# First two down parts of a feed-forward stage as seven products of half blocks

## The chip, the cores and the metric

One NeuronCore of a Trainium2 chip runs the whole program. The metric is the device time of one execution in microseconds (us), lower is better.

## The reference, cut to what matters

A vector of 512 tokens by 1024 features passes through eight stages: feed-forward (stages 0, 2, 3, 5, 7) and mixers (1, 4, 6). The change concerns the feed-forward stages, which all compute

```
def swiglu_ffn(x, norm, w_gate, w_up, w_down):
    h = rms_norm(x, norm)
    return (jax.nn.silu(h @ w_gate) * (h @ w_up)) @ w_down
```

with `x = x + 0.5 * swiglu_ffn(...)` in four of them and a factor of 1 in the last. The hidden width is 2816. Everything is fp32. The kernel reaches that precision with three fp32r products for each product: an operand is split into a high part (rounded to fp32r) and a low part (the rest), and high by high, low by high and high by low are summed in PSUM.

## The kernel before, in words

**Queues.** Each engine's instructions are written by Python generators that yield a planned time ("tick", one tick is three matmuls of 512 columns) before each step; `weave` merges the generators of an engine in order of these ticks. So the yields set the order of an engine's instructions, and nothing else: what starts when is decided on the chip by semaphores.

**Weights.** A weight chunk is 512 KB (128 partitions by 1024 fp32) in one of 12 buffers (`k_raw`, `k_xraw`). SyncE's queue loads it. Before use it is split: ScalarE writes the high part (`k_wh` or `k_xwh`, L842 in `act_weights`), VectorE the rest (`k_wl` or `k_xwl`, L867 in `dve_weights`). There are four such pairs, freed when TensorE has spent a chunk. A buffer is free again when VectorE has split it. The class `Plan` hands out buffers and pairs in program order.

**Gate and up products.** The hidden columns are cut into six blocks (four of 512, two of 384). For a block, gate and up are two halves of one 2x2 block product (input features and token halves by weight halves) that is done with seven half-size products instead of eight (Winograd's form, P1 to P7). The products need sums of weight quarters: T2 = B12+B11+B22 for P6 (and, with B21 added, for P4), T1 for P5, T3 for P7. A sum is made by loading one quarter and adding others with an accumulating DMA from GpSimd's queue (L876, `pool_sum`), or by a VectorE sum of two buffers (L848, `mix`). In block 1 before the change, T1 is loaded as B12 and B11 is added by DMA; in blocks 2 to 5 T1 = T2 - B22 is a VectorE sum.

**Down.** The hidden activations h of a block are turned by TensorE (`pe_turns`, L1107), and ScalarE and VectorE write high and low parts of the turned tiles (`k_h`, L1118 and L1126). Blocks 0 and 1 together are down part 0, blocks 2 and 3 part 1, blocks 4 and 5 part 2. Each part is a plain product: 8 output tiles by 8 hidden tiles (6 in part 2), each three matmuls of 512 tokens, in eight weight chunks. VectorE adds each output tile to x (L967, `dve_residual`). Part 0 is done between P7 and P5 of block 2, part 1 between P7 and P5 of block 4, part 2 at the end.

Of the kernel before, what the change touches and what calls it, by code (L numbers as in the profile page):

```python
# [12 lines left out]
P = 128  # L13
T = 512
# [16 lines left out]
NB = len(BLOCKS)  # L31

# [298 lines left out]
Y_BANKS = {0: (0, 1), 1: (6, 7), 2: (2, 3), 3: (4, 5), 4: (2, 3), 5: (4, 5)}  # L331
SOURCE = {"P1": "B11", "P2": "B21", "P3": "B22", "P4": "T2", "P5": "T1", "P6": "T2", "P7": "T3"}


def weight_steps(st):
# [3 lines left out]
    out = {(b, n): dict(loads=[], adds=[], more=[], pre=[], post=[], gone=[]) for b in range(NB) for n in SOURCE}  # L339
    for b in range(NB):  # L340
# [5 lines left out]
        }.get(b, ((b - 1, "P5"), (b, "P1"), (b - 1, "P4"), (b - 1, "P3")))  # L346
# [17 lines left out]
        if b > 1:  # L364
# [7 lines left out]
        for n in ("P2", "P3", "P4", "P5", "P7"):  # L372
            at(n)["gone"].append((b, SOURCE[n]))
    return out


def weight_pieces(st, b, name, spec):

    wg, wu, _, l, _ = FFN[st]
    out = []  # L380
    for h in range(2):
        key = lambda b, n: (st, b, n, h)

        def src(b, n):
            c0, w = BLOCKS[b]
# [14 lines left out]
def plan_ffn(p, st, keep, seven):  # L400
# [22 lines left out]
    def down(g):  # L423
        last = g == NB // 2 - 1
        if last and not keep:
            p.close_pair()
# [3 lines left out]
        if last:  # L430
            steps = [(kb, m) for kb in range(2) for m in (0, 2, 4)] + [(0, 6), (1, 6)]
            home = {0: (4, 5), 2: (0, 1), 4: (2, 3), 6: (4, 5)}
        else:
            steps = [(kb, q + m) for q in (0, 4) for kb in range(2) for m in (0, 2)]
            home = {0: (0, 1), 2: (2, 3), 4: (0, 1), 6: (2, 3)}
        for kb, m in steps:
            ck = (st, "down", g, kb, m)
            src = (wd, l, BLOCKS[b0][0] + kb * nf * P, nf, m * P, 256)
            c = p.chunk(p.now, 2 * nf, nf, 256, ((ck, src),), ck, gone=(ck,), ext=not last or keep)
# [6 lines left out]
        if last and not keep:  # L446
            p.close_units()

    for b, name in ORDER:
        if name == "down":  # L450
            down(b)
        else:
            product(b, name)
# [7 lines left out]
class Kernel:  # L461
# [26 lines left out]
    def memory(self):  # L488
# [34 lines left out]
        self.H = [(tile(h, 2 * i), tile(h, 2 * i + 1)) for i in range(8)]  # L523
        self.SX = {}
# [216 lines left out]
    def pe_down(self, e, st, part, last):  # L741
        nf = BLOCKS[2 * part][1] // P
        steps = [(kb, m) for kb in range(2) for m in (0, 2, 4)] + [(0, 6), (1, 6)]
        if not last:
            steps = [(kb, q + m) for q in (0, 4) for kb in range(2) for m in (0, 2)]
        for kb, m0 in steps:
# [15 lines left out]
    def pe_ffn(self, e, st):  # L762
        left = {"P1": "A11", "P2": "A12", "P3": "S4", "P4": "A22", "P5": "S1", "P6": "S2", "P7": "S3"}
        for b, name in ORDER:
            if name == "down":
                yield from self.pe_down(e, st, b, b == NB // 2 - 1)
# [117 lines left out]
    def pool_ended(self, e):  # L884
        for c in self.p.chunks:
            for x in c.more:
                yield c.split + 2.4
# [91 lines left out]
    def pe_ffn_norm(self, e, st):  # L979
        yield self.at[st]["start"] + 12.9  # L980
# [8 lines left out]
    def act_ffn_norm(self, e, st):  # L989
        yield self.at[st]["start"] + 13.9  # L990
# [4 lines left out]
    def dve_ffn_norm(self, e, st):  # L995
        yield self.at[st]["start"] + 14.5
# [27 lines left out]
    def dve_ffn_sums(self, e, st, q):  # L1024
# [44 lines left out]
        yield t["S4"] + 6.3  # L1069
# [14 lines left out]
    def turn_tick(self, st, b, q):  # L1084
        return self.at[st][b, "P3"] + 18.0 + 3.0 * q

    def h_key(self, b, q):
        nf = BLOCKS[b][1] // P
        return b // 2, (b % 2) * nf + q

    def pe_turns(self, e, st, b):

        for q in range(BLOCKS[b][1] // P):
            yield self.turn_tick(st, b, q)
            bank = self.bank[6 + q % 2]
            if q > 1:
                e.wait_ge(*self.dve.sig(("xl", st, "h") + self.h_key(b, q - 2)))
# [3 lines left out]
            else:  # L1101
                nf = BLOCKS[b - 1][1] // P
                back = nf - 2 + q if nf % 2 == 0 else nf - 1 - q
                e.wait_ge(*self.dve.sig(("xl", st, "h") + self.h_key(b - 1, back)))
# [5 lines left out]
    def act_turns(self, e, st, b):  # L1110
        for q in range(BLOCKS[b][1] // P):
            yield self.turn_tick(st, b, q) + 0.5
            part, i = self.h_key(b, q)
            e.wait_ge(*self.pe.sig(("turn", st, b, q)))
            if part:
                nf = BLOCKS[2 * part - 2][1] // P
                e.wait_ge(*self.pe.sig(("done", st, "down", part - 1, 7)))
            e.activation(self.H[i][0], self.bank[6 + q % 2], ACT.Copy).then_inc(*self.act.up(("xh", st, "h", part, i)))  # L1118
# [12 lines left out]
    def act_copy(self, e, st, b, name, mark, dst, ref):  # L1131
        w, banks = BLOCKS[b][1], self.p.group[st, b, "P1"].banks
        for m in range(2):
            yield self.done_at(st, b, name, m) + 0.0
            e.wait_ge(*self.pe.sig(("done", st, b, name, m)))
            e.wait_ge(*self.sig(ref))
            e.activation(dst[m][:, 0:w], self.bank[banks[m]][:, 0:w], ACT.Copy).then_inc(*self.act.up((mark, st, b, m)))  # L1137

    def act_blocks(self, e, st, b):
# [1634 lines left out]
```

## Time and profile before

| | before |
|---|---|
| runs | 3165.3 us median of 3 (3165.1 to 3166.48) |
| profiled execution, its own time | 3162.72 us |
| its span | 3160.9 us |
| mean granted TensorE clock | 0.997 of full |
| instructions | 37974 |

The span is from the first to the last instruction of the program; 1.8 us of the execution lie around it. "Busy" of TensorE's matmuls (PE) counts an instruction from its start to its last result, and successive matmuls overlap, so busy time near 100% says little about the distance between starts. The distance between starts is read from the order of time (the timeline).

### The profile page before, as it was taken

The page shows a single profiled execution, that of the slowest core. Times are in us where ns is not written, and L with a number is a line of the kernel's source. Part 1 is how long each engine was busy: PE and PEld are TensorE (multiplying, and loading weights), DVE is VectorE, ACT ScalarE, POOL GpSimd, SP SyncE. Part 2 cuts the span into 40 slices and gives each one's busy share as a digit, 9 for nine tenths or more (in the row PEclk, how much of TensorE's full clock was granted, in tenths as well). Part 3 has the DMA queues.
Part 4 walks back from the last instruction along what each step waited for, and adds up shares of the span by engine and source line. Part 5 has one row for each costly group of instructions (what it writes and reads, how often), then busy time and mean ns, then how long its engine had stood idle before and what let it go on. Part 6 is the DMA issues. An engine that isn't in the chain of part 4 may idle for free.

```text
span 3160.9 us, 37974 instructions
## 1 busy us (share of the span) xinstructions
PE 3110.3 (98%) x15130; PEld 2571.4 (81%) x15130; DVE 2060.4 (65%) x3190; ACT 1617.1 (51%) x2515; POOL 320.2 (10%) x358
## 2 busy tenths in 40 slices
PE   9999999999999999999999999999999999999998
PEld 7789877778887888788987777887889877787887
DVE  7665778745476657756578855457575666785656
ACT  6443568644354436534467754345353556564434
POOL 2110020100021001201001100002010100021100
PEclk9999999999999999999999999999999999999999
DMA  9844341322399456957233322369572554289552
GB/s 262 206 111 110 100 117 61 107 80 87 100 240 221 118 127 180 232 134 174 67 108 93 90 87 80 94 186 233 135 171 71 109 89 68 67 237 220 118 130 69
DMA packets 297586, 417.95 MB, mean 132 GB/s; under 512 B 15424, under 2 KB 199232, under 8 KB 297408
## 3 DMA queue, kind: packets, MB, share of 16 engines
q1 hardware_dynamic: 234592, 298.62, 31.6%
q0 software_dynamic: 62240, 116.02, 20.1%
q8 instruction: 118, 1.93, 0.3%
q10 hardware_dynamic: 576, 0.88, 0.1%
q14 instruction: 60, 0.49, 0.0%
HBM read 407.07 MB, written 2.10 MB: 129 GB/s over the span
## 4 chain that ended last, share of the span: by engine, by line
PE 79%; DVE 9%; DMA 7%; ACT 4%; issue 1%; POOL 0%; DVEq 0%; SPq 0%; ACTq 0%; POOLq 0%
PE bank L656 24%; PE bank L668 14%; PE bank L661 14%; PE bank L670 10%; PE bank L663 10%; DMA k_xraw<-in_ffn_w_gate 4%; DVE k_wl L867 2%; PE bank L1489 1%; PE bank L1107 1%; DMA k_xraw<-in_ffn_w_up 1%; PE bank L1538 1%; PE bank L1522 1%; ACT k_wh L842 1%; DMA k_xraw<-in_w_gate 1%; PE bank L1791 1%
## 5 line engine op out<-in xcount | busy, mean ns | idle before, releaser
L867 DVE TENSOR_TENSOR k_wl<-k_raw,k_wh 128x1024 fp32r<-128x1024 f32 (+1 forms) x314 | 369.9, 1178 | 272.5 <-ACT k_wh L842 270.8
L842 ACT ACTIVATE k_wh<-k_xraw 128x1024 fp32r<-128x1024 f32 (+1 forms) x302 | 300.2, 995 | 446.4 <-PE bank L668 211.9
L842 ACT ACTIVATE k_wh<-k_raw 128x1024 fp32r<-128x1024 f32 (+1 forms) x314 | 320.9, 1022 | 399.8 <-PE bank L668 298.8
L867 DVE TENSOR_TENSOR k_wl<-k_xraw,k_wh 128x1024 fp32r<-128x1024 f32 (+1 forms) x302 | 343.0, 1143 | 176.0 <-ACT k_wh L842 175.4
L656 PE MATMUL bank<-k_xh,k_wh 128*128 128x512 f32 x968 | 395.8, 409 | 0.0
L668 PE MATMUL bank<-k_xh,k_wl 128*128 128x512 f32 x968 | 378.6, 391 | 0.1
L661 PE MATMUL bank<-k_xl,k_wh 128*128 128x512 f32 x968 | 377.7, 390 | 0.0
L670 PE MATMUL bank<-k_wl,k_S 128*128 128x512 f32 (+1 forms) x732 | 272.7, 373 | 15.4 <-ACT k_sc L1137 13.0
L656 PE MATMUL bank<-k_wh,k_S 128*128 128x512 f32 (+1 forms) x732 | 274.4, 375 | 0.0
L656 PE MATMUL bank<-k_h,k_wh 128*128 128x512 f32 x696 | 272.4, 391 | 0.0
L668 PE MATMUL bank<-k_h,k_wl 128*128 128x512 f32 x696 | 271.1, 390 | 0.0
L663 PE MATMUL bank<-k_wh,k_S 128*128 128x512 f32 (+1 forms) x732 | 271.1, 370 | 0.0
L661 PE MATMUL bank<-k_h,k_wh 128*128 128x512 f32 x696 | 270.9, 389 | 0.0
L656 PEld LDWEIGHTS bank<-k_xh,k_wh 128*128 128x128 f32 x968 | 182.3, 188 | 45.2 <-issue 10.1
L668 PEld LDWEIGHTS bank<-k_xh,k_wl 128*128 128x128 f32 x968 | 181.7, 188 | 40.2 <-DVE k_wl L867 0.5
L661 PEld LDWEIGHTS bank<-k_xl,k_wh 128*128 128x128 f32 x968 | 182.3, 188 | 33.4 <-issue 1.0
L670 PE MATMUL bank<-k_wl,k_uf 128*128 128x512 f32 (+1 forms) x528 | 200.2, 379 | 4.3 <-ACT k_sc L1137 2.5
L656 PE MATMUL bank<-k_wh,k_uf 128*128 128x512 f32 (+1 forms) x528 | 202.9, 384 | 0.0
L876 POOL DMA_DIRECT2D k_xraw<-in_ffn_w_gate x82 | 100.5, 1305 | 979.7 <-DMA k_xraw<-in_ffn_w_up 500.2
L663 PE MATMUL bank<-k_wh,k_uf 128*128 128x512 f32 (+1 forms) x528 | 199.3, 377 | 0.4 <-DVE k_uf L943 0.4
L967 DVE SCALAR_TENSOR_TENSOR k_x<-bank,k_x 128x512 f32<-128x512 f32 x160 | 110.0, 689 | 118.0 <-PE bank L668 117.8
L670 PEld LDWEIGHTS bank<-k_wl,k_S 128*128 128x128 f32 x732 | 137.5, 188 | 37.7 <-ACT k_sc L1137 15.1
(424 smaller groups left out, 6547.8 us busy)
## 6 DMA issues: line engine op xcount, KB each, us to landing
k_raw<-in_w_in SPq DMA_DIRECT2D x153, 512.0 KB, 3.7
k_xraw<-in_ffn_w_up SPq DMA_DIRECT2D x65, 512.0 KB, 8.6
k_xraw<-in_ffn_w_gate POOLq DMA_DIRECT2D x54, 512.0 KB, 9.7
k_xraw<-in_ffn_w_gate SPq DMA_DIRECT2D x51, 512.0 KB, 7.1
k_xraw<-in_ffn_w_down SPq DMA_DIRECT2D x49, 512.0 KB, 4.4
k_xraw<-in_ffn_w_up POOLq DMA_DIRECT2D x30, 512.0 KB, 10.6
k_raw<-in_w_out SPq DMA_DIRECT2D x28, 512.0 KB, 3.4
k_raw<-in_ffn_w_gate POOLq DMA_DIRECT2D x22, 512.0 KB, 12.6
```

Of the source, the lines that this page charges most:

```text
L656: e.matmul(o, a[0], b[0], start=first, stop=False, skip_group_check=True)
L661: e.matmul(o, wh, xl, start=False, stop=False, skip_group_check=True)
L663: e.matmul(o, xl, wh, start=False, stop=False, skip_group_check=True)
L668: i = e.matmul(o, wl, xh, start=False, stop=end, skip_group_check=True)
L670: i = e.matmul(o, xh, wl, start=False, stop=end, skip_group_check=True)
L842: e.activation(self.pair[c.pair][0][:, 0:n], self.unit[c.src][:, 0:n], ACT.Copy).then_inc(*self.act.up(("wh", c.i)))
L867: e.tensor_tensor(lo[:, 0:n], self.unit[c.src][:, 0:n], hi[:, 0:n].bitcast(F32), ALU.subtract).then_inc(*self.dve.up(("wl", c.i), ("split" ...
L876: e.dma_start(dst, src, accum_op=ALU.add).then_inc(*self.steps[f"sum{uid}"].up(count))
L967: e.scalar_tensor_tensor(out=self.X[m], in0=self.bank[bank], scalar=scale, in1=self.X[m], op0=ALU.mult, op1=ALU.add).then_inc(*self.dve.up ...
L1107: i = e.transpose(bank[:, t * P:(t + 1) * P], u[:, q * P:(q + 1) * P], self.ident)
L1489: i = e.matmul(outs[s], x[rows, qcols], y[rows, kcols], start=n == 0, stop=n == 2, skip_group_check=True)
L1522: j = e.transpose(self.bank[6][:, kt * P:(kt + 1) * P], p[:, kt * P:(kt + 1) * P], self.ident)
```

## The change

1. Parts 0 and 1 of down are done in Winograd's form too: outputs are cut into two halves of four tiles, tokens into two halves of 256, hidden features into two halves (the two blocks). Seven products (`DOWN_ORDER`), each of 16 (output tile, hidden tile) pairs, each three matmuls of 256 tokens. Six weight buffers' worth of quarter sums (T1, T2, T3) are made by accumulating DMA.
2. The turned h of parts 0 and 1 is kept as plain fp32 (`k_hf`); the seven activation operands are made from it one by one: four VectorE sums of 1024 (L1240), seven high parts on ScalarE, seven rests on VectorE (L1223, L1226). Each product's result goes into x by VectorE as soon as it is done (L1263), 14 instructions for a part.
3. The part is moved behind P3 of block 2 (or 4), where the other products of that block are done.
4. Block 1's T1 becomes a VectorE sum: B22 is loaded where B12 was, and the add by DMA goes.
5. Some thirty yields get other offsets, in all stages.

```diff
-        out += [(b, "P6"), (b, "P2"), (b, "P7")] + [(b // 2 - 1, "down")] * (b % 2 == 0) + [(b, "P5")]
-        out += [(b + 1, "P1")] * (b + 1 < NB) + [(b, "P4"), (b, "P3")]
+        out += [(b, "P6"), (b, "P2"), (b, "P7"), (b, "P5")] + [(b + 1, "P1")] * (b + 1 < NB) + [(b, "P4"), (b, "P3")]
+        out += [(b // 2 - 1, "down")] * (b % 2 == 0)
...
-        if b > 1:
+        if b > 0:
             out[begin1]["loads"].append((b, "B22", "B22"))
             at("P6")["loads"].append((b, "T1", None))
             at("P6")["post"].append((b, "T1", "T2", "B22", ALU.subtract, None))
...
+    for b, before in (("D0", 2), ("D1", 4)):
+        at = lambda n: out[b, n]
+        for n, piece in (("P1", "B11"), ("P2", "B21"), ("P3", "B22")):
+            at(n)["loads"].insert(0, (b, piece, piece))
+        out[before, "P4"]["loads"].append((b, "T2", "B12"))
+        out[before, "P4"]["adds"].append((b, "T2", "B11"))
+        out[before, "P3"]["adds"].append((b, "T2", "B22"))
+        at("P1")["loads"].append((b, "T1", "B12"))
+        at("P1")["adds"].append((b, "T1", "B11"))
+        at("P2")["loads"].append((b, "T3", "B12"))
+        at("P2")["adds"].append((b, "T3", "B22"))
+        at("P6")["more"].append((b, "T2", "B21"))
...
+    def pe_down(self, e, st, part):
+
         nf = BLOCKS[2 * part][1] // P
...
+        for n, name in enumerate(DOWN_ORDER):
+            g = self.p.group[st, "down", part, name]
+            t = g.at
+            hi, lo = self.OP[n % 2]
+            for h, c in enumerate(g.chunks):
+                wh, wl = self.parts(c)
+                for m in range(2):
+                    cols = slice(m * P, (m + 1) * P)
+                    for k in range(nf):
+                        yield t
+                        t += HALF
+                        s = slice(256 * k, 256 * k + 256)
...
+    def down_tick(self, st, part, n):
+
+        return self.at[st]["down", part] + (8.5 * (n - 1) + 0.9 if n > 1 else -10.7 + 2.2 * n)
...
+            if n > 1:
+                e.wait_ge(*self.pe.sig(("done", st, "down", part, DOWN_ORDER[n - 2], 1)))
...
     def pe_ffn_norm(self, e, st):
-        yield self.at[st]["start"] + 12.9
+        yield self.at[st]["start"] + 18.9
```

TensorE's queue at the start of part 0 in stage 0, before (the rows repeat for 192 matmuls; `k_h` is the turned h, `k_wh` and `k_wl` the weight's parts):

```order
L656 MATMUL bank<-k_h,k_wh 128x512
L661 MATMUL bank<-k_h,k_wh 128x512
L668 MATMUL bank<-k_h,k_wl 128x512
L656 MATMUL bank<-k_h,k_wh 128x512
L661 MATMUL bank<-k_h,k_wh 128x512
```

And now (336 matmuls):

```order
L692 MATMUL bank<-k_h,k_wh 128x256
L697 MATMUL bank<-k_h,k_wh 128x256
L704 MATMUL bank<-k_h,k_wl 128x256
L692 MATMUL bank<-k_h,k_wh 128x256
L697 MATMUL bank<-k_h,k_wh 128x256
```

What moved: there are 144 more matmuls in a part, each half as wide.

VectorE's queue in the same part, before (`k_x` is the residual, L967 the sum into it):

```order
L867 TENSOR_TENSOR k_wl<-k_xraw_82,k_wh 128x1024
L967 SCALAR_TENSOR_TENSOR k_x<-bank,k_x 128x512 x2
L867 TENSOR_TENSOR k_wl<-k_xraw_77,k_wh 128x1024
L967 SCALAR_TENSOR_TENSOR k_x<-bank,k_x 128x512 x2
L867 TENSOR_TENSOR k_xwl<-k_raw,k_xwh 128x1024
```

And now, two and a half of the seven products (L922 is the weight's rest, L1240 a sum of activations, L1223 and L1226 an operand's rest, L1263 the sum into the residual):

```order
L1240 TENSOR_TENSOR k_sc<-k_sc,k_hf 128x1024
L1263 SCALAR_TENSOR_TENSOR k_x<-bank,k_x 128x2x256
L922 TENSOR_TENSOR k_wl<-k_xraw_74,k_wh 128x1024
L1263 SCALAR_TENSOR_TENSOR k_x<-bank,k_x 128x2x256
L1223 SCALAR_TENSOR_TENSOR k_h<-k_sc,k_h 128x1024
L922 TENSOR_TENSOR k_wl<-k_xraw_78,k_wh 128x1024
L1263 SCALAR_TENSOR_TENSOR k_x<-bank,k_x 128x2x256
L1240 TENSOR_TENSOR k_sc<-k_sc,k_hf 128x1024
L922 TENSOR_TENSOR k_wl<-k_xraw_80,k_wh 128x1024
L1263 SCALAR_TENSOR_TENSOR k_x<-bank,k_x 128x2x256
L1226 TENSOR_TENSOR k_h<-k_sc,k_h 128x1024
```

What moved: a chunk's split is now followed by a sum into x, and between them stand the rests and sums of the activation operands. From the start of the part to its end the queue holds 14 weight rests, 14 sums into x, 5 operand rests, 3 activation sums and 4 sums of the next block's weights.

## Rows read from the trace of the kernel before

**Rows 1.** The page's busy time, share of the span and instructions

```profile
PE 3110.3 (98%) x15130; PEld 2571.4 (81%) x15130; DVE 2060.4 (65%) x3190; ACT 1617.1 (51%) x2515; POOL 320.2 (10%) x358
```

**Rows 2.** The chain that ended last, by engine

```profile
PE 79%; DVE 9%; DMA 7%; ACT 4%; issue 1%; POOL 0%; DVEq 0%; SPq 0%; ACTq 0%; POOLq 0%
```

**Rows 3.** Windows in stage 2: length, busy by engine, clock, DMA share, GB/s

```profile
1009.80:1053.30 43.50, 43.50 (x194) 36.02 (x193) 14.83 (x16) 8.97 (x9) 4.75 (x4) 1.00 0.54 128
...
970.00:980.00 10.00, 6.80 (x29) 5.28 (x28) 5.18 (x6) 5.02 (x8) 1.18 (x1) 0.96 1.11 249
1053.30:1075.00 21.70, 21.70 (x97) 18.00 (x96) 14.72 (x15) 10.83 (x12) 1.18 (x1) 1.00 0.31 86
```

**Rows 4.** TensorE's starts (us), durations: down part 0, stage 2

```profile
1032.88 0.39 PE L656 MATMUL bank<-k_h,k_xwh 128*128 128x512 f32 x1
...
1034.92 0.39 PE L656 MATMUL bank<-k_h,k_xwh 128*128 128x512 f32 x1
```

**Rows 5.** The same, block 5 of stage 2, ten matmuls apart

```profile
1189.74 0.33 PE L670 MATMUL bank<-k_xwl,k_S 128*128 128x384 f32 x1
...
1191.47 0.33 PE L656 MATMUL bank<-k_wh,k_S 128*128 128x384 f32 x1
```

**Rows 6.** Twenty narrow matmuls in attention, and their weight loads (PEld)

```profile
1765.60 2.39 PE L1538 MATMUL bank<-k_pt,k_qkva 128*128 128x128 f32 x20
...
1765.37 2.42 PEld L1538 LDWEIGHTS bank<-k_pt,k_qkva 128*128 128x128 f32 x20
```

**Rows 7.** Groups by shape: count, busy us, mean ns, idle before

```profile
L656 PEld LDWEIGHTS bank<-k_xh,k_wh 128*128 128x128 f32 x968 | 182.3, 188 | 45.2 <-issue 10.1
...
L867 DVE TENSOR_TENSOR k_wl<-k_xraw,k_wh 128x1024 fp32r<-128x1024 f32 x213 | 258.5, 1222 | 123.9 <-ACT k_wh L842 123.6
...
L967 DVE SCALAR_TENSOR_TENSOR k_x<-bank,k_x 128x512 f32<-128x512 f32 x160 | 110.0, 689 | 118.0 <-PE bank L668 117.8
```

**Rows 8.** VectorE in order of time, stage 2

```profile
979.60 1.23 DVE L867 TENSOR_TENSOR k_xwl<-k_xraw,k_xwh 128x1024 fp32r<-128x1024 f32 x1 [0.21 <-ACT k_xwh L842]
980.74 1.28 DVE L1180 TENSOR_TENSOR k_sc<-bank,k_sc 128x512 f32<-128x512 f32 x2
```

**Rows 9.** TensorE around its stall in P5 of block 1, stage 2

```profile
975.08 0.39 PE L663 MATMUL bank<-k_wh,k_S 128*128 128x512 f32 x1
978.67 0.50 PE L670 MATMUL bank<-k_wl,k_S 128*128 128x512 f32 x1 [3.20 <-ACT k_sc L1137]
...
979.77 0.63 PE L670 MATMUL bank<-k_wl,k_uf 128*128 128x512 f32 x1
980.20 0.63 PE L656 MATMUL bank<-k_wh,k_uf 128*128 128x512 f32 x1
```

**Rows 10.** ScalarE in the same stall

```profile
971.97 0.58 ACT L1137 ACTIVATE k_sc<-bank 128x512 f32<-128x512 f32 x1
977.08 1.06 ACT L842 ACTIVATE k_wh<-k_xraw 128x1024 fp32r<-128x1024 f32 x1 [4.52 <-DMA k_xraw<-in_ffn_w_gate]
978.04 0.58 ACT L1137 ACTIVATE k_sc<-bank 128x512 f32<-128x512 f32 x1
```

**Rows 11.** GpSimd's adds that precede it: two for T1, one for T2

```profile
940.22 2.18 POOL L876 DMA_DIRECT2D k_raw<-in_ffn_w_gate  x1
943.23 1.18 POOL L876 DMA_DIRECT2D k_xraw<-in_ffn_w_gate  x1 [0.83 <-issue]
...
955.11 1.18 POOL L876 DMA_DIRECT2D k_xraw<-in_ffn_w_gate  x1 [3.38 <-DVE k_wl L867]
```

**Rows 12.** TensorE's waits, whole program: total us, times, longest

```profile
PE bank L670 <- ACT k_sc L1137: 15.5, 6, 3.2
...
PE bank L670 <- DVE k_wl L867: 4.2, 6, 1.3
```

**Rows 13.** DMA queues, 940 to 980 us: adds (q0), loads (q1)

```profile
q0 software_dynamic: 2951, 5.69, 77.0%
q1 hardware_dynamic: 2323, 4.47, 33.3%
```

More of the change, by code:

```diff
@@ L331 @@
 Y_BANKS = {0: (0, 1), 1: (6, 7), 2: (2, 3), 3: (4, 5), 4: (2, 3), 5: (4, 5)}
+DOWN_ORDER = ("P1", "P2", "P6", "P5", "P7", "P3", "P4")
 SOURCE = {"P1": "B11", "P2": "B21", "P3": "B22", "P4": "T2", "P5": "T1", "P6": "T2", "P7": "T3"}
 def weight_steps(st):
-    out = {(b, n): dict(loads=[], adds=[], more=[], pre=[], post=[], gone=[]) for b in range(NB) for n in SOURCE}
+    out = {(b, n): dict(loads=[], adds=[], more=[], pre=[], post=[], gone=[]) for b in (*range(NB), "D0", "D1") for n in SOURCE}
     for b in range(NB):
@@ L423, in down, with down_last @@
     def down(g):
-        last = g == NB // 2 - 1
-        if last and not keep:
+        nf = BLOCKS[2 * g][1] // P
+        at["down", g] = p.now
+        for name in DOWN_ORDER:
+            at["down", g, name] = p.now
+            cs = []
+            for s in weight_pieces(st, f"D{g}", name, steps_of[f"D{g}", name]):
+                cs.append(p.chunk(p.now, 2 * nf * HALF, nf, 256, ext=True, **s))
+                p.now += 2 * nf * HALF
+            banks = swapped(st, (4, 5) if name in ("P1", "P6", "P7", "P4") else (0, 1))
+            p.fill((st, "down", g, name), at["down", g, name], banks, cs)
+            drain(banks, [("dve", ("dn", st, g, name, t)) for t in range(2)])
+    def down_last():
+        g = NB // 2 - 1
+        if not keep:
             p.close_pair()
@@ L429, in down @@
         at["down", g] = p.now
[L430 to L436, printed above, removed]
+        home = {0: (4, 5), 2: (0, 1), 4: (2, 3), 6: (4, 5)}
+        for kb, m in [(kb, m) for kb in range(2) for m in (0, 2, 4)] + [(0, 6), (1, 6)]:
             ck = (st, "down", g, kb, m)
             src = (wd, l, BLOCKS[b0][0] + kb * nf * P, nf, m * P, 256)
-            c = p.chunk(p.now, 2 * nf, nf, 256, ((ck, src),), ck, gone=(ck,), ext=not last or keep)
+            c = p.chunk(p.now, 2 * nf, nf, 256, ((ck, src),), ck, gone=(ck,), ext=keep)
             banks = swapped(st, home[m])
@@ L445, in down @@
                 drain(banks, [("dve", ("x", st, g, m + i)) for i in range(2)])
-        if last and not keep:
+        if not keep:
             p.close_units()
     for b, name in ORDER:
-        if name == "down":
+        if name != "down":
+            product(b, name)
+        elif b == NB // 2 - 1:
+            down_last()
+        else:
             down(b)
-        else:
-            product(b, name)
     p.side = 0
@@ new lines, in dve_operand_sums @@
+    def dve_operand_sums(self, e, st, part, name):
+        before = {"P7": "P5", "P3": "P6"}.get(name)
+        for i, (t, out, x, y, op) in enumerate(self.down_source(st, part, name)[1]):
+            yield self.at[st]["down", part] + t
+            if name == "P6":
+                e.wait_ge(*self.dve.sig(("h", st, 2 * part + 2, 3 - 2 * i)))
+                e.wait_ge(*self.act.sig(("hf", st, part, 7)))
+            else:
+                e.wait_ge(*self.dve.sig(("xl", st, "O", part, before)))
+            if i:
+                e.wait_ge(*self.dve.here())
+            e.tensor_tensor(out, x, y, op).then_inc(*self.dve.up(("os", st, part, name, i)))
@@ L1476, in dve_halves @@
         for t, (q, k, ql, kl, qh, kh) in enumerate(a["q"]):
[L1477 removed]
+            yield a["start"] + (8 * t - 1.5 if t else -2.0) * a["step"]
             e.wait_ge(*self.act.sig(("kh", st, kind, t)))
```

195 lines of the change are left out of this document (136 added, 59 removed), and 2 rows, old and new, of the table at.

## The prediction

> **What bounds the kernel now.** I first read the page's busy times [rows 1] and its chain [rows 2]: matmuls are busy 98% of the span and hold 79% of the chain, VectorE is busy 65% and holds 9%, transfers 7%. So TensorE's own work sets the time, and a change pays if it takes matmul time away without making TensorE wait. Then I read the place of the change. Down part 0 of stage 2 runs from 1009.8 to 1053.3 us [rows 3]: 192 matmuls of 512 columns in 43.5 us, VectorE busy 14.8, ScalarE 9.0, DMA share 0.54. TensorE waits for nothing there. In order of time, nine starts are 2.04 us apart [rows 4], so one matmul costs 0.2267 us, and 192 make 43.5: the part is pure matmul time. Last I read what TensorE waits for in the whole program [rows 12]: 15.5 us for ScalarE's copies out of PSUM, in six places, and 4.2 us for weight rests. The longest is in P5 of block 1 of stage 2, at 975.1 us [rows 9]. ScalarE's queue explains it [rows 10]: before the copy that TensorE wants stands a weight split that waited 4.52 us for an add by DMA. This is T2's add of block 1, issued at 955.11 and landed when the split began, at 977.08; ahead of it in the same queue went T1's two adds [rows 11]. DMA is saturated there: share 1.11 at 249 GB/s [rows 3].
>
> **Part by part: matmuls.** A part had 192 matmuls of 512 columns and gets 7 x 16 x 3 = 336 of 256. No row shows a lone 128-row matmul of 256 columns in fp32r, so I bound it. Matmuls of 384 columns start 1.73/10 = 0.173 us apart [rows 5]. From 512 to 384 the step is 0.0534 us for 128 columns, so 256 columns come to 0.120 on the straight line. Below, weight loads limit: twenty loads of 128 columns take 2.42 us, one alone 0.19 [rows 6], so they follow each other at (2.42 - 0.19)/19 = 0.117. Above, 0.173 holds, since a narrower matmul is not dearer. I take 0.120: both neighbours on the line are measured and the floor lies under it. A part is then 336 x 0.120 = 40.3 us, 3.2 less; ten parts (two in each of five stages) give **-32**. At the floor it is 39.3 and -42; break-even is 43.5/336 = 0.1295 us.
>
> The Trainium skill (TensorE: Matmul & The Clock Gate, LDWEIGHTS) puts a load of P columns at P/1.2 ns, 107 ns for 128, and says fp32 gets no fast load. By that page's gap of N/2.4 + 2.5 ns a matmul of 256 columns would come every 109 ns, a part would last 36.7 us and ten parts would save 68; the rows at 512 and 384 columns lie 11 ns over that formula, so the sum does not use it.
>
> **VectorE in a part.** By the queue's order it holds, between start and end of a part, 14 weight rests, 5 operand rests, 3 activation sums and 4 weight sums, 26 instructions of 1024, and 14 sums into x of 512. Alone one takes 1.222 and 0.689 us [rows 7]; behind one another 1.14 (979.60 to 980.74) and 1.28 - 0.69 = 0.59 [rows 8]. So 26 x 1.14 + 14 x 0.59 = 37.9 us of 40.3, or 94%; with the times alone it would be 41.4. Before it was 14.8 of 43.5. This is the tightest point. Each product lasts 48 x 0.120 = 5.8 us. Its operand's high part waits for the end of the product two before (ScalarE, about 1.06), then VectorE's rest needs 1.22: about 3.4 us are left for VectorE being late. The weight splits run up to three chunks (8.6 us) ahead, and the block before uses VectorE less (14.7 of 21.7 us [rows 3]). So short lateness is absorbed, but some will reach TensorE where a sum into x waits for a product and holds the rests behind it. I allow 1.0 us a part (0 to 3): **+10**.
>
> ScalarE gets 14 splits and 7 high parts of about 1.06, 22 us of 40: hidden. The turning of blocks 2 and 4 moves into the end of the part, with the same transposes; it costs what it cost.
>
> **Transfers.** A part had 8 loads and gets 12 loads and 10 adds, 22 x 0.524 = 11.5 MB instead of 4.2. In the saturated 40 us, adds took 77.0% of all engines for 5.69 MB and loads 33.3% for 4.47 MB [rows 13], that is 2.8 us an add and 1.6 us a load, with 110% reached. So a part needs (12 x 1.6 + 10 x 2.8)/1.10 = 43 us of a DMA that is full, in 40.3. The products before lend time: from 1053.3 to 1075.0 the share is only 0.31 [rows 3], and those products now stand ahead of the part. For the two windows together: other work 0.54 x 43.5 + 0.31 x 21.7 - 8 x 1.6 = 17.4, plus 47, over 1.10, is 59 us in 62. It fits, barely, if loads are early: buffers for T1 and T3 come free two to four products before they are needed. I put no cost here, and keep up to 3 us a part for the range.
>
> **Block 1's T1.** Two adds (2 x 2.8 = 5.6 us) leave the queue ahead of T2's add. It would land near 971.5, before ScalarE comes to that split at 972.5, so the stall goes. Of the 15.5 us [rows 12] one wait of 2.5 is at the start of the program and stays; 13 are of this kind over five stages. After it the clock shows 0.96 [rows 3] and matmuls start 0.43 apart instead of 0.227 [rows 9]: eight of them, 1.6 us, in four stages, 6 more. Of these 19 us I take four fifths, since the new sum makes T2's last add issue some 2 us later: **-15**. VectorE pays 2 x 1.14 us in block 1, hidden.
>
> **Other offsets** reorder single instructions in all stages. TensorE's waits for reasons other than the above are small [rows 12]; I take 0, with 6 either way.
>
> **Sum.** 3162.7 (profiled execution) - 32 - 15 + 10 = 3125.7. The runs' median is 2.6 above the profiled execution, so the forecast is **3128 us**.
>
> **The rivals.**
> - *The parts run at VectorE's or the transfers' pace, not slower than before* (2 to 4 us lost a part beyond my allowance). For: 94% of VectorE, 59 of 62 us of DMA. Against: 8.6 us of lead. It gives 3128 + 10 x 2 to 10 x 3.2, so 3148 to 3160. Chance 0.20.
> - *Slower: VectorE's queue becomes the bound of a part.* One mechanism: a sum into x waits for its product, the operand's rest stands behind it, the next product waits for the rest, and this repeats seven times. It decides once a product takes over 43.5 + 1.5 (the stall relief per part) = 45.0 us / 7 = 6.4 us instead of 5.8. At 7.0 us a part is 49: 10 x 8.7 more than the 40.3, 3165.3 - 32 - 15 + 87 = 3205. Chance 0.07.
> - *Slower: weight loads bound a part.* A load shows 188 ns [rows 7], and if none overlapped the next, 336 would take 63.2 us, 19.7 more than before: 3165 + 197 - 15 = 3347. Against: rows 6 show 0.117 between loads. The Trainium skill (Trainium Kernel Development and Optimization, Best Practices) says to judge nearness to the limit by the share of LDWEIGHTS, not of matmuls, which is 81% here [rows 1] and would pass 100% in a part. Chance 0.03.
> - *Slower: adds of narrow weights (runs of 256 columns, 1 KB) cost by the run.* Then an add is 5.6 us, and the two windows need (17.4 + 19 + 56)/1.10 = 84 us in 62: 22 late a part, about 3340. No add of this shape is in the trace. Chance 0.03.
> - *The change does nothing* (within 0.2%, 6.3 us, about what a measurement of this kernel can tell from none): 4.7 us lost a part beyond 40.3. Chance 0.05.
>
> **How the numbers follow.** My forecast (3108 to 3146: the pitch between 0.117 and 0.122, 0 to 2 us lost a part, relief of 8 to 19, offsets of 6) has 0.62. The first rival has 0.20, the three slower ones 0.13, no change 0.05. The range 3106 to 3160 holds the first two, 0.82; the slower ones are left out. Faster 0.82, same 0.05, slower 0.13.
>
> **What the profile would show.** Right: in a part 336 matmuls 0.120 us apart, the part 40 to 42 us plus 1.9 of turning; VectorE over 90% busy in it; no wait of TensorE for ScalarE's copy in P5 of block 1, and clock 1.00 there. Wrong: TensorE waiting in a part for `k_h` (operand rests) or `k_wl`, or VectorE and ScalarE for adds of w_down; starts over 0.1295 us apart; the stall of block 1 still there.

## The result, and the profile after

| | before | after |
|---|---|---|
| median | 3165.89 us (4 runs, 3165.1 to 3166.63) | 3116.15 us (4 runs, 3110.49 to 3119.66) |
| profiled execution, its own time | 3162.72 us | 3119.66 us |
| its span | 3160.9 us | 3117.9 us |
| mean granted TensorE clock | 0.997 | 0.994 |

The ratio is 0.9841 (95% interval 0.9824 to 0.9858): 1.6% faster. The forecast was 3128 us, in a range of 3106 to 3160; the change gained 49.7 us where 37 were forecast.

The page of the profile after, busy time and the chain that ended last, to be set beside [rows 1, 2]:

```profile
PE 3080.8 (99%) x16570; PEld 2622.7 (84%) x16570; DVE 2241.9 (72%) x3350; ACT 1746.8 (56%) x2645; POOL 436.7 (14%) x448
...
PE 86%; DVE 7%; ACT 4%; DMA 3%; issue 1%; POOL 0%; DVEq 0%; SPq 0%; ACTq 0%
```

TensorE's part of the chain rose from 79% to 86% and the transfers' fell from 7% to 3%: less of the time ends in a wait. VectorE has 181 us more to do, and its share of the chain fell all the same.

Windows of the kernel after in stage 2 (length, busy by engine, clock, DMA share, GB/s): the place of block 1's old stall, part 0 and part 1.

```profile
966.00:976.00 10.00, 10.00 (x46) 8.29 (x45) 6.84 (x8) 6.67 (x10) 0.00 (x0) 1.00 0.57 164
1022.40:1064.00 41.60, 41.60 (x349) 41.58 (x348) 40.02 (x43) 21.18 (x22) 9.81 (x8) 1.00 0.99 226
1132.40:1175.10 42.70, 41.80 (x350) 41.60 (x349) 39.69 (x45) 20.25 (x22) 10.16 (x9) 1.00 1.02 218
```

Part 0 now takes 41.6 us, with transposes inside that stood in later products before, against 43.5 [rows 3]. VectorE is busy 40.0 of 41.6 us (96%), DMA is full at 0.99, and TensorE still has no idle time. Part 1 is 1.1 us longer and has 0.9 us of idle time. Block 1's stall, 3.2 us at a DMA share of 1.11 [rows 3, 9], is gone: TensorE is busy 10.0 of 10.0 us, and DMA has air at 0.57.

TensorE in order of time in part 0 of stage 2 (start, duration), every third matmul; the ones between are the other two of each triple:

```profile
1040.05 0.28 PE L692 MATMUL bank<-k_h,k_wh 128*128 128x256 f32 x1
...
1043.65 0.28 PE L692 MATMUL bank<-k_h,k_wh 128*128 128x256 f32 x1
```

Between the two rows lie ten triples, 30 matmuls, in 3.60 us: 0.120 us each, the value on the straight line through [rows 4, 5].

TensorE's waits over the whole kernel after (total us, times, longest), to be set beside [rows 12]:

```profile
PE bank L1633 <- DVE k_sm L1738: 4.5, 6, 0.8
PE bank L2154 <- DVE k_ycat L1796: 3.3, 1, 3.3
PE bank L1666 <- ACT k_pt L1776: 3.2, 5, 2.2
PE bank L1167 <- DVE k_h L1272: 2.3, 3, 1.1
...
PE bank L704 <- DVE k_x L1263: 0.9, 1, 0.9
...
PE bank L697 <- DVE k_h L1223: 0.6, 1, 0.6
```

The 15.5 us for ScalarE's copies `k_sc` are gone in this trace. The wait of 2.5 us at the start of the program, which the prediction said would stay, is gone too: here TensorE comes to it late, after a stretch at half clock (see e3). It is back in e3 and e9, where the clock holds. What the ten parts brought in their place is 2.3 + 0.9 + 0.6 = 3.8 us: transposes that wait for turned rests (L1272), and one wait each for a sum into x (L1263) and an operand's rest (L1223). From first to last matmul the ten parts take 421.4 us, where ten of 41.6 are 416.0: 5.4 us were lost in them, all in part 1 of the five stages.

### The profile page after: what moved, and what is told of

Read it like the earlier page. It is cut to its first block, busy times and chain, and to the rows that moved or that the text cites. A ratio compares the mean times of both kernels' runs of the same rounds, so it can differ in the third digit from the quotient of the medians.

```text
span 3117.9 us, 41438 instructions
## 1 busy us (share of the span) xinstructions
PE 3080.8 (99%) x16570; PEld 2622.7 (84%) x16570; DVE 2241.9 (72%) x3350; ACT 1746.8 (56%) x2645; POOL 436.7 (14%) x448
## 4 chain that ended last, share of the span: by engine, by line
PE 86%; DVE 7%; ACT 4%; DMA 3%; issue 1%; POOL 0%; DVEq 0%; SPq 0%; ACTq 0%
PE bank L692 26%; PE bank L704 13%; PE bank L697 13%; PE bank L706 12%; PE bank L699 12%; PE bank L1633 2%; PE bank L1167 1%; DVE k_wl L922 1%; PE bank L1682 1%; DMA k_raw<-in_ffn_w_gate 1%; PE bank L1666 1%; ACT k_wh L897 1%; PE bank L1935 1%; DMA k_raw<-in_w_down 0%; DMA k_raw<-in_ffn_w_up 0%
## 5 line engine op out<-in xcount | busy, mean ns | idle before, releaser
L922 DVE TENSOR_TENSOR k_wl<-k_raw,k_wh 128x1024 fp32r<-128x1024 f32 (+1 forms) x319 | 376.2, 1180 | 275.0 <-ACT k_wh L897 273.7
L897 ACT ACTIVATE k_wh<-k_raw 128x1024 fp32r<-128x1024 f32 (+1 forms) x319 | 326.8, 1024 | 382.1 <-PE bank L704 253.6
L897 ACT ACTIVATE k_wh<-k_xraw 128x1024 fp32r<-128x1024 f32 (+1 forms) x342 | 342.6, 1002 | 312.6 <-PE bank L706 166.4
L922 DVE TENSOR_TENSOR k_wl<-k_xraw,k_wh 128x1024 fp32r<-128x1024 f32 (+1 forms) x342 | 391.9, 1149 | 157.5 <-ACT k_wh L897 157.0
L692 PE MATMUL bank<-k_h,k_wh 128*128 128x256 f32 (+1 forms) x1056 | 325.3, 308 | 0.0
L704 PE MATMUL bank<-k_h,k_wl 128*128 128x256 f32 (+1 forms) x1056 | 322.2, 305 | 0.9 <-DVE k_x L1263 0.9
L697 PE MATMUL bank<-k_h,k_wh 128*128 128x256 f32 (+1 forms) x1056 | 321.9, 305 | 0.6 <-DVE k_h L1223 0.6
L692 PEld LDWEIGHTS bank<-k_xh,k_wh 128*128 128x128 f32 x968 | 182.7, 189 | 45.6 <-issue 10.4
L704 PEld LDWEIGHTS bank<-k_h,k_wl 128*128 128x128 f32 x1056 | 201.6, 191 | 10.0 <-DVE k_x L1263 1.1
L697 PEld LDWEIGHTS bank<-k_h,k_wh 128*128 128x128 f32 x1056 | 201.7, 191 | 8.8 <-DVE k_h L1223 0.8
L692 PEld LDWEIGHTS bank<-k_h,k_wh 128*128 128x128 f32 x1056 | 201.7, 191 | 7.9
L692 PE MATMUL bank<-k_wh,k_uf 128*128 128x512 f32 (+1 forms) x528 | 200.4, 379 | 0.0
```

The lines of the kernel that those rows point to most:

```text
L692: e.matmul(o, a[0], b[0], start=first, stop=False, skip_group_check=True)
L697: e.matmul(o, wh, xl, start=False, stop=False, skip_group_check=True)
L704: i = e.matmul(o, wl, xh, start=False, stop=end, skip_group_check=True)
L897: e.activation(self.pair[c.pair][0][:, 0:n], self.unit[c.src][:, 0:n], ACT.Copy).then_inc(*self.act.up(("wh", c.i)))
L922: e.tensor_tensor(lo[:, 0:n], self.unit[c.src][:, 0:n], hi[:, 0:n].bitcast(F32), ALU.subtract).then_inc(*self.dve.up(("wl", c.i), ("split" ...
```

## The experiments

Each run was timed beside the kernel before, on the same chip; medians of 4 to 7 runs. Side by side with each other ran e1, e2, e3 and e5; e6, e7, e9 and e10; e8 and e11; e12 and e13. Other differences reach over two such groups, in which the kernel before took 3163.46 to 3166.32 us: they are good to about 3 us at best.

### e1: block 1's T1 by DMA again

```diff
-        if b > 0:
+        if b > 1:
             out[begin1]["loads"].append((b, "B22", "B22"))
```

> The changed kernel with block 1's T1 made by load and add in DMA again, all else as changed. Theory A (the gain beyond the matmuls is the stall of block 1, which the sum on VectorE removes): the wait in P5 of block 1 is back in all five stages, about 20 us with its slow clock, so 3136 us, 3130 to 3142. Theory B (the moved offsets of the feed-forward stages removed that stall, not T1): no wait comes back, 3116 us, within 3.

Measured: 3141.11 us (3137.68 to 3143.83), ratio 0.9928 (0.9914 to 0.9941). A: with the rest of the change in place, making T1 on VectorE is worth 25 us (3141.11 - 3116.15; this goes over two groups). TensorE's waits for `k_sc` in it, where the kernel before has 15.5 us in 6 places [rows 12]:

```profile
PE bank L706 <- ACT k_sc L1284: 18.6, 7, 5.0
```

### e2: the kernel before, with T1 as a VectorE sum

```diff
-        if b > 1:
+        if b > 0:
             out[begin1]["loads"].append((b, "B22", "B22"))
```

> The kernel before with nothing but block 1's T1 as a VectorE sum. Theory A: P5 and P4 of block 1 lose their excess (20.8 us over five stages in the trace of before), so 3145 us, 3141 to 3152. Theory B: the offsets were needed, less than 5 us gained, 3161 to 3166.

Measured: 3145.2 us (3144.8 to 3146.65) against 3163.46 for the kernel before in the same call: -18.3, ratio 0.9943 (0.9931 to 0.9956). A again. Of the waits only the one at the start of the program is left:

```profile
PE bank L670 <- ACT k_sc L1137: 2.5, 1, 2.5
```

15.5 - 2.5 = 13.0 us of waiting went, and 18.3 us of time. Most of the other 5.3 are the slow starts behind the stalls [rows 9]: in the kernel before, the clock is at half for 3.4 us behind four of the five (at 98.5, 979.1, 2204.5 and 2876.9 us), where 6.8 us of time are lost at most, and in e2 behind none.

### e5: the new down parts alone

The changed kernel with T1 by DMA (as e1) and with all other offsets as before: the start, the mixers and the feed-forward steps outside the parts.

> The kernel before with the parts as seven products and their place alone: T1 of block 1 by DMA, and every offset outside the parts as before. Theory A: 10 x 3.2 us of matmul time less, and the stall of block 1 stays: 3134 us, 3130 to 3140. Theory B: the parts need the other offsets to run unhindered: 3145 us or more, with waits inside the parts.

Measured: 3139.83 us (3133.53 to 3144.77), ratio 0.9922 (0.9909 to 0.9934): the parts alone bring 23.6 us, at the slow end of what was expected, and A. TensorE waits for `k_sc` 16.6 us in 6 places, about as in the kernel before. e1 differs from e5 in the offsets outside the parts alone, and took 1.3 us more, less than either spreads.

### e3 and e13: the old offsets at the start of the program

```diff
-            yield (-8.9, -8.8, -4.5, -8.9, -4.0, -0.9, 1.0, 0.0)[k]
+            yield (-8.9, -8.8, -4.5, -5.9, -1.0, -0.9, 1.0, 1.1)[k]
             self.act_entry(e, 0, k)
...
-            yield (-3.8, -2.6, -6.0, -6.2, -4.6, -3.7, 1.2, 1.3)[k]
+            yield (-6.8, -5.6, -6.0, -6.2, -4.6, -3.7, 1.2, 1.3)[k]
...
-            yield (-8.8, -8.7, -5.9, -5.8, -0.9, -0.8, 4.1, 1.2)[k]
+            yield (-8.8, -8.7, -5.9, -5.8, -0.9, -0.8, 1.1, 1.2)[k]
```

> The changed kernel with the offsets of the program's first 30 us (ScalarE's and VectorE's entry and squares) as before. The profiled execution of the changed kernel has its TensorE clock at half from 12.1 to 36.0 us, after two waits of 1.65 us, and loses about 12 us there. Theory C (the new start offsets make these waits): granted clock 0.997 in every run and 3109 us, 3105 to 3112. Rival D (the half clock at the start comes by chance of the execution, as the spread of the changed kernel's runs suggests): median 3116 us, within 3, and the clock between 0.994 and 0.997 again.

Measured: 3110.67 us (3109.06 to 3119.0), ratio 0.9838 (0.9825 to 0.9852). The median speaks for C, but the interval overlaps that of the changed kernel, and the profiled execution, 3119.0 us, lies outside C's 3105 to 3112. Its trace shows why, and what the theories had left out. Part 1 of stage 0 ends in a wait of TensorE, and behind that the clock falls. VectorE, ScalarE and TensorE of e3 in order of time:

```profile
294.27 0.96 DVE L922 TENSOR_TENSOR k_wl<-k_xraw,k_wh 128x768 fp32r<-128x768 f32 x1 [4.30 <-ACT k_wh L897]
...
298.48 0.69 DVE L1272 TENSOR_TENSOR k_h<-bank,k_h 128x512 fp32r<-128x512 f32 x1
```

```profile
293.40 0.84 ACT L897 ACTIVATE k_wh<-k_xraw 128x768 fp32r<-128x768 f32 x1 [6.42 <-DMA k_xraw<-in_ffn_w_up]
```

```profile
299.22 0.66 PE L1167 MATMUL bank<-k_const,k_sc 128*128 128x128 f32 x4 [2.69 <-DVE k_h L1272]
```

Read from the bottom: TensorE's transposes waited 2.69 us for a turned rest. That rest stood in VectorE's queue behind the splits and sums of block 5's weights, which began late, since VectorE had been idle 4.30 us for ScalarE, and ScalarE 6.42 us for a transfer. So VectorE is the messenger; a late add by DMA (GpSimd issued adds of the up weights at 287.22 and 290.30 us) began it. Over that execution these waits came to 8.4 us in 4 places.

To settle the start, the changed kernel and e3 ran once more side by side.

> The changed kernel unchanged, side by side with the next run, since its four runs (3110.5 to 3119.7) and e3's four (3109.1 to 3119.0) overlap. S (the new offsets at the start let the clock fall there: so far in all three traces that have them): median 3115 to 3120, granted clock from 8 to 40 us under 0.95. N (chance): as e3, 3110 to 3113.

> e3 again: the changed kernel with the old offsets at the start. S: median 3109 to 3112, that is 4 to 9 us under the run before, and clock from 8 to 40 us at 0.97 or more (nine traces with the old offsets so far, one of them at 0.89). N: no difference between the two runs beyond 2 us.

Measured: the changed kernel 3114.8 us (3110.63 to 3115.96), ratio 0.9837 (0.9823 to 0.985); e3's kernel 3111.39 (3108.77 to 3118.53), ratio 0.9834 (0.9818 to 0.985). The difference of 3.4 us lies between S and N, and the two ratios are nearly equal. The trace of e13, alone among ten with the old offsets, shows a long stretch at half clock too. Windows from 8 us on of the changed kernel's profiled execution, then of e13:

```profile
8.00:20.00 12.00, 8.70 (x30) 7.19 (x30) 6.55 (x10) 8.55 (x15) 0.00 (x0) 0.67 1.05 404
20.00:40.00 20.00, 20.00 (x80) 17.48 (x80) 14.89 (x29) 10.62 (x20) 1.19 (x1) 0.60 0.59 165
```

```profile
8.00:20.00 12.00, 10.42 (x37) 8.68 (x37) 5.78 (x8) 8.68 (x15) 0.00 (x0) 0.64 1.05 407
20.00:40.00 20.00, 20.00 (x79) 17.44 (x80) 17.10 (x32) 11.11 (x22) 1.19 (x1) 0.62 0.55 162
```

The second row of each is pure loss: TensorE is busy for the whole 20 us and gets through about 80 matmuls, where e3 gets through 104. What it costs can be read off where part 0 of stage 0 begins: at 145.7 us in e3 and 145.5 in e9, with full clock, but at 152.2 in e13, the same kernel as e3, and at 153.1, 151.4 and 151.6 in the changed kernel, e12 and e8. So the half clock costs 6 to 8 us in an execution where it lasts for 17 to 24 us.

### e8 and e9: the old offsets in stage 6 as well

e9 puts stage 6's six offsets back on top of e3, e8 on top of the changed kernel, so the two differ in the start alone. Two of the lines:

```diff
-        start, end = at["start"] + 59.4, at["xbc"][1].at + 8.4
+        start, end = at["start"] + 58.6, at["xbc"][1].at + 7.6
...
-                yield self.at[st]["gelu", j][0].at + 15.6 + 0.1 * m
+                yield self.at[st]["gelu", j][0].at + 16.4 + 0.1 * m
```

> The changed kernel with the old offsets at the start and also in stage 6, where the changed one's profiled execution takes 5.6 us more than before (waits of 3.3 us for k_ycat and 2.2 us for k_pt, clock at half in two short stretches at 2610 to 2630 us). C (the new offsets of stage 6 cost that): 5 us under e3, 3105 to 3107. D (the waits only change place, or come with the other timing of what stands ahead): 3109 to 3113.

> Is it the new offsets at the start of the program that let TensorE's clock fall there? So far all eight traces with the old offsets show a granted clock of 1.00 from 8 to 40 us, and both with the new ones (the changed kernel 0.63, e1 0.89) do not. This run keeps the new start and puts only stage 6 back, so it differs from e9 (median 3111.2) in the start alone. S (the new start costs it): the granted clock from 8 to 40 us is under 0.95 and the median 2 to 9 us over e9, 3113 to 3120. N (chance): clock 1.00 there and 3109 to 3113.

Measured: e9 3111.22 us (3107.62 to 3116.14), ratio 0.9835 (0.9821 to 0.9848), as e3: D. The wait of 3.3 us for `k_ycat` is still there, so these offsets did not make it. e5, with every old offset, lacks it, so one of the others did; which one was not tried. e8 3119.44 us (3115.58 to 3124.07), ratio 0.9855 (0.9839 to 0.9872): 8.2 us over e9, though that goes over two groups (by the ratios it is 6) and the intervals overlap a little, and granted clock 0.73 from 8 to 40 us. S.

Granted clock from 8 to 40 us in all traces of this study:

```
old offsets at the start: before 1.00, e2 1.00, e3 1.00, e5 1.00, e6 1.00, e7 1.00, e9 1.00, e10 1.00, e11 0.89, e13 0.63
new offsets at the start: after 0.63, e12 0.73, e8 0.73, e1 0.89
```

TensorE in the changed kernel before the fall, its idle times in brackets:

```profile
9.86 0.50 PE L706 MATMUL bank<-k_wl,k_uf 128*128 128x512 f32 x1 [1.65 <-DVE k_wl L922]
...
12.71 1.91 PE L2642 MATMUL bank<-k_one,k_sc 128*128 128x32 f32 x8 [1.65 <-ACT k_sc L991]
```

The first wait, for a weight rest, all executions have. The second, for a square of x, is in all four traces with the new offsets and in none of the ten with the old: ScalarE now writes three more high parts of x at 10.63 us and its first square at 12.04, where e3 has its first square at 7.43.

But it is not what lets the clock fall in each of them. In e12 the clock falls at 11.4 us, and the second wait only begins at 12.0. What stands before that fall, and before the two with the old offsets (e11 at 11.6 us, e13 at 11.4), is this:

```profile
10.57 0.50 PE L706 MATMUL bank<-k_wl,k_uf 128*128 128x512 f32 x1 [2.31 <-DVE k_wl L922]
...
11.25:11.50 0.25, 0.25 (x3) 0.09 (x1) 0.25 (x1) 0.25 (x1) 0.00 (x0) 0.75 1.04 402
```

```profile
10.07 0.50 PE L706 MATMUL bank<-k_wl,k_uf 128*128 128x512 f32 x1 [2.02 <-DVE k_wl L922]
```

```profile
8.42 0.50 PE L692 MATMUL bank<-k_wh,k_uf 128*128 128x512 f32 x1 [1.70 <-ACT k_uf L979]
...
10.59 0.50 PE L706 MATMUL bank<-k_wl,k_uf 128*128 128x512 f32 x1 [1.03 <-DVE k_wl L922]
```

So e12 (first) and e11 (second) had a longer first wait, 2.31 and 2.02 us where the eight with full clock have 1.02 to 1.48, and e13 (last) had another of 1.70 us ahead of it. These lengths vary between executions of one kernel (1.65 us in the changed kernel's trace, 2.31 in e12's). The new offsets add the later wait to that chance. That they make a fall more likely is what four of four against two of ten say; why the clock falls is not shown beyond that.

### e6 and e7: more work for VectorE in a part

```diff
+                if True:
+                    e.tensor_tensor(lo, src, hi.bitcast(F32), ALU.subtract).then_inc(*self.dve.up())
+                    e.wait_ge(*self.dve.here())
                 e.tensor_tensor(lo, src, hi.bitcast(F32), ALU.subtract).then_inc(*self.dve.up(("xl", st, "O", part, name)))
```

e7 has `if name in ("P5", "P3"):` in place of `if True:`. Both stand on e3.

> Is VectorE really at its limit in a part? The changed kernel with the old offsets at the start of the program (run e3, median 3110.7 us), and in each of the ten parts six of the seven operand rests are done twice, the second behind the first: 6 x 1.14 to 1.22 = 6.8 to 7.3 us more VectorE work a part. A (VectorE at 94% is nearly the bound): 37.9 + 7 = 45 us of VectorE work for 40.3 us of products, so about 4.6 us late a part, less what the products before and behind the part lend (2 us or so): +25 to +46 us, 3136 to 3157, and TensorE waits in the parts for the operand rests. B (the 8.6 us of lead absorb it, VectorE catches up in the products behind the part): under +6 us, 3111 to 3117.

> As the run before, but only the rests of two products (P5 and P3) are done twice: +2.3 to 2.4 us of VectorE a part, 40.3 us of work in 40.3 us. A: just at the limit, +0 to +10 us, so 3111 to 3121. B (lead absorbs it): 3111, no difference from e3. If the first of these two runs costs 25 us or more and this one under 5, the margin of VectorE in a part lies between 2.4 and 7 us.

Measured: e6 3155.13 us (3152.14 to 3161.29), ratio 0.997 (0.9959 to 0.9981), so 44.5 over e3: A. e7 3115.03 us (3113.68 to 3123.08), ratio 0.9851 (0.9837 to 0.9864), 4.4 over e3: within A's range, and not far from none. Its trace has waits for the doubled rest (L1229) all the same, 4.9 us in 6 places. Parts 0 and 1 of stage 2 in e6:

```profile
1022.50:1068.50 46.00, 43.39 (x352) 42.36 (x351) 45.62 (x48) 21.57 (x23) 9.82 (x8) 1.00 0.89 204
1137.20:1184.80 47.60, 43.88 (x350) 42.38 (x349) 47.25 (x53) 21.37 (x23) 9.93 (x9) 1.00 0.94 197
```

VectorE is busy 45.6 of 46.0 us and sets the pace. From first to last matmul the ten parts take 464.6 us in e6, 43 more than in the changed kernel: nearly all of the 44.5 lies in them. And VectorE does so by the second rival's mechanism, in some of the products. TensorE in e6, then VectorE, which has the sum into x (L1266) ahead of the operand's rest (L1227, and L1229 once more):

```profile
1042.22 0.39 PE L697 MATMUL bank<-k_h,k_wh 128*128 128x256 f32 x1 [0.99 <-DVE k_h L1229]
...
1049.22 0.39 PE L697 MATMUL bank<-k_h,k_xwh 128*128 128x256 f32 x1 [0.98 <-DVE k_h L1229]
```

```profile
1046.09 0.68 DVE L1266 SCALAR_TENSOR_TENSOR k_x<-bank,k_x 128x512 f32<-128x512 f32 x1
1046.69 1.22 DVE L1227 TENSOR_TENSOR k_h<-k_sc,k_h 128x1024 fp32r<-128x1024 f32 x1
1047.94 1.23 DVE L1229 TENSOR_TENSOR k_h<-k_sc,k_h 128x1024 fp32r<-128x1024 f32 x1
```

The two waits are 7.00 us apart, against 5.8 between products without the extra work. Two of this part's products last 7.0 us, as the rival said, the others 5.8 to 6.5, and a whole part 45.4 to 47.3 us, not 49. So VectorE's margin in a part lies between 2.4 us, which cost 4.4 in all, and 7 us, which cost 44.5.

### e10: three quarters of the down sums left out

```diff
         uid, count, waits, (name, l, r0, kt, c0, cols) = x
+        if name.endswith("w_down"):
+            kt = 1
```

> Are the transfers that I put at no cost late at the end of a part? The changed kernel with the old offsets at the start (e3, median 3110.7, its profiled execution 3119.0 with 8.4 us of waits of the transposes in part 1 for the turned rests), and the adds by DMA of down weights bring only one of their four row groups: three quarters of each of these sums is left out, so about 10 x 3/4 of an add's load a part is gone, with the same instructions on every engine. T (the waits in part 1 begin with a late transfer, ScalarE's weight split stands behind it, then VectorE and the transposes): the waits of TensorE for k_h of the turned rests fall under 1 us, its clock does not fall near the end of part 1, the median is 3103 to 3109. V (VectorE's own load makes them late): the same waits stay, 3110 to 3112.

Measured: 3106.81 us (3106.42 to 3108.43), ratio 0.9821 (0.9807 to 0.9834), 3.9 under e3, whose kernel it stands on, and 4.4 under e9, which ran beside it: T in time. All four runs are faster than each of the eight of e3 and e13, though the intervals of the ratios overlap. The same two parts of stage 2 in it:

```profile
1011.60:1053.20 41.60, 41.60 (x350) 41.60 (x349) 40.02 (x44) 21.24 (x22) 7.67 (x7) 1.00 0.70 169
1121.50:1163.10 41.60, 41.60 (x349) 41.60 (x349) 41.09 (x47) 20.79 (x22) 8.09 (x8) 1.00 0.66 148
```

VectorE is as busy as before, DMA at 0.70 and 0.66 instead of 0.99 and 1.02, and part 1 is down to 41.6 us with no idle time. One wait of 1.5 us for a turned rest is left in the program, where I expected less than 1, and e9 has no more than that either. What tells T from V is the length of the parts: nine of ten last 41.6 us in e10, and the ten have lost 1.7 us together, against 10.9 in e3, 4.9 in e9 and 5.8 in e13, with VectorE's work the same. The chain of waits of the changed kernel through part 1 of stage 2 (start, length, what) tells the same:

```profile
1146.09 14.52 DMA k_raw<-in_ffn_w_gate
...
1160.91 7.10 DMA k_raw<-in_ffn_w_up
...
1168.04 0.85 ACT k_xwh L897
...
1168.92 0.97 DVE k_xwl L922
...
1169.91 1.83 DVE k_xraw L903 x2
...
1173.20 0.61 DVE k_h L1272
...
1173.86 0.66 PE bank L1167 x4
```

Two adds by DMA, 14.5 and 7.1 us from issue to landing, for block 5's weights and behind the down sums in the same queue, then ScalarE's split, VectorE's queue, and the transposes.

### e11: the turning of block 4 later

```diff
-        return (self.at[st]["down", b // 2 - 1] + 52.0 if b in (2, 4)
+        return (self.at[st]["down", b // 2 - 1] + (59.0 if b == 4 else 52.0) if b in (2, 4)
```

> The changed kernel with the old offsets at the start (e3, median 3110.7), and the twelve transposes of block 4 of each feed-forward stage seven ticks later, behind the last product of part 1 instead of inside it. The part 2 that needs them is three products or more away. T (the transposes in P4 of part 1 wait for turned rests that stand behind late weight splits): the waits for k_h of the turned rests go (8.4 us in e3's profiled execution, 1.5 to 2.3 in others), P4 of part 1 is no longer than 5.9 us, and the median is 1 to 4 us less, 3107 to 3110. V (VectorE or ScalarE is then late in the products of block 5 instead, where copies out of PSUM wait for the turning): no gain, 3110 to 3116, with waits of TensorE for k_sc in block 5.

Measured: 3111.54 us (3107.48 to 3113.03), ratio 0.9827 (0.9812 to 0.9842): no gain on e3. A miss for T, though not as V had it. The transposes stand behind the part now, and they wait there for the same rests:

```profile
PE bank L1167 <- DVE k_h L1272: 3.6, 4, 1.8
```

TensorE's wait for `k_sc` is 2.6 us in 2 places, what e9 has too. This stall, which begins with a late transfer, moved with the instruction that meets it. Part 1 of stage 2 without its transposes is a clean measure of 336 matmuls, and the other four stages give the same 40.3 us:

```profile
1125.40:1165.70 40.30, 40.30 (x338) 40.30 (x337) 37.31 (x42) 18.96 (x19) 10.02 (x9) 1.00 1.07 230
```

## Why the prediction was right, and where its sizes were off

**Matmuls, -32: right.** 0.120 us between starts of 256 columns, so a product takes 5.76 us and a part 40.3, and that is what part 1 lasts in e11. What the two other prices would have made is excluded, 0.117 as well as 0.173. The Trainium skill (TensorE: Matmul & The Clock Gate, Back-to-back issue gap: N/2.4 + 2.5 ns for a matmul by itself) gives 109 ns; at 256 columns too the rows lie 11 ns over it.

**VectorE, +10: oversized.** The load was right, 94% said and 96% shown, and so was the thought that lead absorbs it. The allowance was not: the ten parts lose 5.4 us in the changed kernel's trace and 4.0 in e12's, and most of that begins with a late transfer. It depends on the execution, up to 10.9 in e3. The allowance was taken from nothing that was measured. e7 bounds what VectorE has to spare: 2.4 us more work a part cost 4.4 us in all ten. With 7 us more a part (e6) the second rival's mechanism came true, in two products of the seven, and the program was still faster than before.

**Transfers, 0: slightly wrong.** "It fits, barely" is what the windows show, 0.99 and 1.02. But in part 1 adds land late, by up to 6.4 us of ScalarE's waiting (e3), and this reaches TensorE. e10 puts the price of the down sums' load at about 4 us over the program. Adds of 1 KB runs cost little more by the byte: the DMA queues in part 0 of stage 2, adds and loads, were

```profile
q0 software_dynamic: 3282, 4.36, 64.1%
q1 hardware_dynamic: 3272, 5.00, 34.9%
```

that is 0.641 x 41.6/(4.36/0.524) = 3.2 us an add and 1.5 us a load; the sum had 2.8 and 1.6. The fourth rival, which needed 5.6 us an add, is out.

**Parts together.** -32 + 10 = -22 was forecast and e5 measured -23.6. That the two are so close is in part luck. Its ten parts lose 5.8 us, so -26 would be expected. The missing 2 to 3 us have candidates in its trace: 1.1 us more of waiting for `k_sc` (16.6 against 15.5), and a clock that fell for 3.4 us in seven places instead of four, up to 1.7 us each. Its three runs with a mean clock of 0.997, that of the kernel before, took 3133.5 to 3140.2 us, the two with 0.995 took 3139.8 and 3144.8. That these make up the difference is argued, not shown.

**Block 1's T1, -15: undersized.** The term was four fifths of 19. Alone it measured -18.3, all of the 19: I took off a fifth for T2's last add being issued later, and no trace shows that this costs anything. On top of the parts it is worth more, 25.0 (e1 against the changed kernel, 3141.11 - 3116.15). Parts alone and T1 alone make -41.9; the whole change makes -49.7. So the two help each other by some 7 us, a difference that reaches over two groups of runs and so is uncertain by several us. The traces bear it out: TensorE's waits in e1 are 20.4 us more than in the changed kernel (46.1 against 25.7 us in all), those of the kernel before 12.7 more than in e2 (38.8 against 26.1). e1's waits for `k_sc` are 18.6 us with one of 5.0, where the kernel before had 15.5 and 3.2, and its waits for turned rests 5.4 instead of 2.3. Why the stall grows beside the parts stays open, and some of it may be the execution's: the waits for turned rests alone range from 1.1 to 8.4 us in the other traces with the parts.

**Other offsets, 0 with 6 either way: right in size, with a loss at the start inside.** Where the clock falls at the start for 17 us or more it costs 6 to 8 us of that execution; between medians the new offsets at the start cost 3.4 us (e12 against e13) to 8.2 us (e8 against e9). Stage 6's change nothing. All offsets together made 1.3 us (e1 against e5), so the rest of them seem to give some of this back. The traces show a place: TensorE's waits for `k_sm` in stages 1 and 4 are 9.3 us in e5 and 4.6 in e1. Those of the other mixers and of the feed-forward steps were not tried apart.

**Weight loads one behind another, 188 ns each: excluded.** Loads are busy 41.58 of 41.60 us in a part, and matmuls still start 0.120 us apart, so loads overlap each other. Whether the last of the 0.120 is the matmul's own or the load's, whose floor was read as 0.117, no run tells. The Trainium skill (Trainium Kernel Development and Optimization, Best Practices) judges distance to the limit by the share of LDWEIGHTS together with the useful work done (MFU). By that share a part is at its limit, and this trace agrees: part 0 lasts what 336 matmuls (40.3) and twelve transposes (1.3) take. But in e6 loads are busy for 42.4 of 46.0 us while VectorE sets the pace, so a high share alone doesn't name the bound.

**The whole.** 12 us lower than forecast: by the runs 1.6 of them from the parts (e5), 3.3 from T1 alone (e2), and some 8 from what both and the offsets make together, which already holds what the half clock at the start takes back. The mechanism was the forecast one; what the sum lacks is a term for T1 and the parts together.

**A version that may beat it.** e3, the changed kernel with the start's old offsets, was faster than the changed kernel both times by the medians (3110.67 against 3116.15, 3111.39 against 3114.8), and e9 than e8 by 8.2. The intervals of all three pairs overlap, and by the ratios the first two differ by 1 us only. So it is likely better, by a few us, and not shown.

## What to carry to other kernels

Price an unseen tile size by the straight line through two measured ones and set bounds from the nearest rows; here that term was exact. An engine at 95% of a stretch cost next to nothing here, where its work is spread and its consumers run behind a lead, but find out how many microseconds of margin are left, by adding work until it breaks. When a wait names an engine, follow that engine's queue back: here VectorE's lateness began with an add by DMA.

## What the runs showed of the hardware that was not expected

TensorE's clock fell to its lower level (1.2 of 2.4 GHz) at the start of the program for 6.8 to 23.9 us in six of fourteen traces, where most falls later in the program lasted 3.4 us. A wait of 1.0 to 2.3 us at about 10 us is in every trace. The eight that kept the full clock have one of 1.0 to 1.5 us there and none over 0.5 us beside it. The six that fell had more waiting near it: 2.0 us in that wait alone (e11), 2.3 (e12), or a second wait of 1.2 to 2.3 us before or behind it (the changed kernel, e1, e8, e13). Each of these waits is short, and the fall that follows lasts up to ten times as long. No run changed one of these waits by itself.

An accumulating transfer takes about twice the engine time of a load of the same bytes (3.2 against 1.5 us for 512 KB), in runs of 1 KB too.
